# Weights streamed in pairs of chunks: one 1 MB load into two slots in place of two 512 KB loads

## The reference

```python
def first_block(x, ...):
    h = rms_norm(x, norm_mix_g[l])
    proj = h @ w_in[l]
    q, k, v, xr, gr, sc_b, sc_c, sc_x, g_pre = jnp.split(proj, offs, axis=-1)
    ...
    x = x + (g_a * y_a + g_b * y_b + g_c * y_c) @ w_out[l]
    h = rms_norm(x, norm_mlp_g[l])
    x = x + jnp.square(jax.nn.relu(h @ w_mlp_up[l])) @ w_mlp_down[l]
    return rms_norm(x, final_g)

def hybrid_layer(x, ...):
    h = rmsnorm(x, g_mix) @ w_in
    ...
    x = x + jnp.concatenate([y_ssd, y_att], axis=-1) @ w_out
    u = rmsnorm(x, g_mlp) @ w_up
    return x + jnp.square(jax.nn.relu(u)) @ w_down
```

## Time and profile before

| | |
|---|---|
| median of three runs | 2666.14 us (2665.62 to 2667.29) |
| the profiled execution | 2667.68 us, its span 2666.0 us |
| TensorE busy | 2656.8 us of the span |
| DVE, ACT busy | 1988.2 us, 1369.1 us |
| granted clock of TensorE | 0.999 |
| read from HBM | 505.08 MB, 191 GB/s over the span |

### The profile page before, as it was taken

One profiled execution on the slowest core, in us unless ns is written; L12 is line 12 of the kernel. 1 busy time (PEld: TensorE's weight loads), 2 busy tenths in 40 slices (PEclk: granted clock), 3 DMA queues, 4 the chain that ended last, 5 costly groups with the idle time before them and its releaser, 6 DMA issues.

```text
span 2666.0 us, 39598 instructions
## 1 busy us (share of the span) xinstructions
PE 2656.8 (100%) x13478; PEld 2243.8 (84%) x13478; DVE 1988.2 (75%) x2876; ACT 1369.1 (51%) x1865; POOL 30.3 (1%) x64
## 2 busy tenths in 40 slices
PE   9999999999999999999999999999999999999999
PEld 7888888888888888888888888888788888888887
DVE  5687876555555778798797577878787977879886
ACT  6455555444444554555554454456555555455453
POOL 0100000000000000000000000000000000000000
PEclk9999999999999999999999999999999999999999
DMA  7655556666665566566566555545555665656565
GB/s 275 227 173 188 185 169 195 207 198 194 204 192 186 177 197 202 185 195 199 187 207 203 189 178 172 175 151 189 171 173 189 199 197 189 205 188 195 186 202 175
DMA packets 141721, 511.06 MB, mean 192 GB/s; under 512 B 16134, under 2 KB 16439, under 8 KB 141464
## 3 DMA queue, kind: packets, MB, share of 16 engines
q1 hardware_dynamic: 136312, 493.86, 57.4%
q0 software_dynamic: 3840, 12.86, 1.5%
q10 hardware_dynamic: 1440, 2.62, 0.3%
HBM read 505.08 MB, written 4.21 MB: 191 GB/s over the span
## 4 chain that ended last, share of the span: by engine, by line
PE 94%; DVE 4%; DMA 1%; ACT 1%; issue 1%; SPq 0%; ACTq 0%; DVEq 0%
PE acc L1952 26%; PE acc L1953 13%; PE acc L1967 5%; PE acc L1984 4%; PE acc L1986 4%; PE acc L1985 4%; PE pS L1984 3%; PE pT L1986 3%; PE pS L1986 3%; PE pT L1984 3%; PE pS L1985 3%; PE pT L1985 3%; PE acc L1968 2%; PE pO L1984 1%; PE pO L1985 1%; PE pO L1986 1%
## 5 line engine op out<-in xcount | busy, mean ns | idle before, releaser
L1104 DVE TENSOR_TENSOR wlo<-raw,whi 128x1024 fp32r<-128x1024 f32 x938 | 1144.3, 1223 | 456.3 <-ACT whi L614 450.5
L614 ACT ACTIVATE whi<-raw 128x1024 fp32r<-128x1024 f32 x938 | 990.5, 1057 | 802.4 <-PE pT L1986 246.7
L1952 PE MATMUL acc<-a_w,whi 128*128 128x512 f32 x2944 | 1046.2, 400 | 0.1
L1953 PE MATMUL acc<-a_w,wlo 128*128 128x256 f32 x2944 | 827.3, 281 | 0.0
L1952 PEld LDWEIGHTS acc<-a_w,whi 128*128 128x128 f32 x2944 | 553.6, 188 | 137.8 <-issue 0.8
L1953 PEld LDWEIGHTS acc<-a_w,wlo 128*128 128x128 f32 x2944 | 556.6, 189 | 0.7
L1967 PE MATMUL acc<-a_w,whi 128*128 128x512 f32 x592 | 214.8, 405 | 0.0
L1968 PE MATMUL acc<-a_w,wlo 128*128 128x256 f32 x592 | 165.9, 280 | 0.0
L825 ACT ACTIVATE t<-acc 128x256 f32<-128x256 f32 x128 | 49.1, 383 | 176.8 <-PE acc L1953 175.1
L1967 PEld LDWEIGHTS acc<-a_w,whi 128*128 128x128 f32 x592 | 111.4, 188 | 27.0 <-issue 2.0
L1500 DVE TENSOR_TENSOR t<-acc,t 128x256 f32<-128x256 f32 x128 | 54.1, 423 | 79.2 <-ACT t L825 79.0
(11 more groups left out here) (496 smaller groups left out, 3962.5 us busy)
## 6 DMA issues: line engine op xcount, KB each, us to landing
raw<-stream SPq DMA_DIRECT2D x938, 512.0 KB, 3.4
gbias<-gateb POOLq DMA_DIRECT2D x12, 256.0 KB, 3.8
X<-x_rows POOLq DMA_DIRECT2D x4, 512.0 KB, 6.8
bias_scratch<-brow POOLq DMA_DIRECT2D x8, 256.0 KB, 5.7
q<-bias_scratch POOLq DMA_DIRECT2D x8, 256.0 KB, 4.0
out<-X ACTq DMA_DIRECT2D x8, 256.0 KB, 5.2
xF<-x SPq DMA_DIRECT2D x6, 256.0 KB, 6.9
bias<-bias_scratch POOLq DMA_DIRECT2D x8, 128.0 KB, 3.6
```

Of the source, the lines that this page charges most:

```text
L614: A(whi[:, slot, :], raw[:, slot, :], ACT.Copy).then_inc(s.hi_done, 1)
L1104: TT(wlo[:, slot, :], raw[:, slot, :], whi[:, slot, :].bitcast(F32), SUB).then_inc(s.lo_done, 1)
L1952: MM(ps, wh, wide[:, k0 + k, :], start=start and k == 0, stop=False, skip_group_check=True)
L1953: last = MM(ps[:, 0:T], wl, wide[:, k0 + k, 0:T], start=False, stop=not start and k == KC - 1, skip_group_check=True)
```

## The change

From chunk 4 on SP loads two chunks with one DMA of 1 MB, into slots 0 and 1 or 2 and 3, and waits for the subtraction of the chunk that lay in the second of the two slots. One semaphore for each pair of slots (`pair_landed`) tells of the landing; ACT's conversions of both chunks and the sums of DVE wait for it. The first four chunks are still loaded one by one. The number of chunks, the ring, the conversions and the products stay as they are.

```diff
+        pair_landed = [ctx.enter_context(nc.semaphore(f"pair_landed{k}")) for k in range(NSLOT // 2)]
...
+            def load_pair(c, slot):
+                sp.dma_start(raw[:, slot:slot + 2, :], stream[ds(c, 2)].rearrange("a p c -> p a c")).then_inc(pair_landed[slot // 2], 16)
+
             whole = CHUNKS // NSLOT
             with sp.Fori(1, whole) as i:
-                for k in range(NSLOT):
-                    sp.wait_ge(s.lo_done, i * NSLOT + (k - NSLOT + 1))
-                    load(i * NSLOT + k, k)
-            for c in range(whole * NSLOT, CHUNKS):
-                sp.wait_ge(s.lo_done, c - NSLOT + 1)
-                load(c, c % NSLOT)
+                for k in range(0, NSLOT, 2):
+                    sp.wait_ge(s.lo_done, i * NSLOT + (k - NSLOT + 2))
+                    load_pair(i * NSLOT + k, k)
+            for c in range(whole * NSLOT, CHUNKS, 2):
+                sp.wait_ge(s.lo_done, c - NSLOT + 2)
+                load_pair(c, c % NSLOT)
...
-                act.wait_ge(landed[slot], c.div(NSLOT).times(16).value(16))
+                if c.least() < NSLOT:
+                    act.wait_ge(landed[slot], 16)
+                else:
+                    act.wait_ge(pair_landed[slot // 2], c.div(NSLOT).times(16).value())
...
-                for e in range(2):
-                    dve.wait_ge(landed[slot + e], 16 * ((c + e) // NSLOT + 1))
+                dve.wait_ge(pair_landed[slot // 2], 16 * (c // NSLOT))
```

## The result

The change makes the kernel slower: 2681.31 us (median of five, 2679.04 to 2683.93) against 2666.14. The ratio is 1.0058, interval 1.0043 to 1.0073. That is outside the range that was forecast, 2665 to 2674, and on the side of rival A, though by another road than A's.

A forecast was written before the change was run, and what follows sets the result against it. TensorE, busy 2656.8 of 2666.0 us, was taken as the bound. Costs of 1.8 us at six crossings and 0 elsewhere were added to the median 2666.1, giving 2667.9, so 2668.0; range 2665.0 to 2674.0.

The forecast's parts named there:

- rival A: All pair loads: the 1 MB load lands late, over 0.2% slower from 5.2 us landing (2671.5), 2692 at 6.5; chance 0.15.
- What bounds the kernel: Whole program: TensorE busy 2656.8 of 2666.0 us at full clock; load changes can only be hidden or make it wait.
- L = 4.6: Pair loads on SP's queue: time from issue to landing of 1 MB taken as 4.6 us, ends 4.4 and 6.5.
- The slope of 6 us for each us of L: Six half changes in the down-projections: each further us from issue to landing costs 6 us more.
- The crossings: Change from a group's first half to its second, six times: late pairs delay DVE's run and TensorE, 1.8 us in all.
- a few tenths vanish: Within a half of the down-projections: TensorE has about 3 us in hand, so small delays disappear.
- The second loop: Successive block pairs in the same slots: landing time + 5.4 against TensorE's 10.2 us; DVE falls back over 4.8 us landing.
- Ordinary stretches: nothing: Judged on an up-projection stretch of the MLP: pair lands 1.05 us early, before TensorE's 5.9 us cover is touched; cost nothing.
- The start: 0, up to 2 us: Chunks 4 to 15: full queue, bytes decide; cost 0, up to 2 us if the first pairs fall behind.
- rival B: The start: squares of X later than reckoned, TensorE waits at 51.94; 2670, still within 0.2%; chance 0.05.
- The bound on conversion 12: The start: chunk 13 lands no later than 38.60, so ACT's conversion of chunk 12 moves by at most 2.7 us.
- D: All pairs: no different from two loads back to back, landing 4.5 us, sum 1.2, 2667.3; chance 0.76 together with the forecast.

The follow-up runs named there:

- e2: Against the changed kernel, each pair's 1 MB issued as two 512 KB loads, still under one joint semaphore; 2677.46 us, ratio 1.0047.
- e6: Against the changed kernel, the pair at each of the six crossings loaded by two single loads, 6 of 467 split; 2676.51 us, ratio 1.0041.
- e9: Against the kernel before, 1 MB loads in the two MLPs alone and not at the six crossings, 250 of 256 pairs; 2666.80 us, ratio 1.0004.
- e5: Against the changed kernel, single loads in both MLPs, pairs kept for chunks 4 to 303 and 560 to 681; 2674.65 us, ratio 1.0031.
- e7: Against the changed kernel, chunks 568 to 573, at the begin of the second layer's mixing, loaded singly; 2676.65 us, ratio 1.0040.
- e1: Against the changed kernel, same trigger, but two 512 KB loads back to back, each with its own semaphore; 2668.57 us, ratio 1.0013.
- e3: Against the changed kernel, the host lays a pair's two chunks so that each partition's 8 KB lie together in memory; 2680.63 us, ratio 1.0054.

## Where the prediction was right and where it failed

- *What bounds the kernel*: right. TensorE's busy time did not move, and only waits could be added.
- *L = 4.6*: failed by 0.3, a term that was mis-sized. Two loads back to back do complete 4.59 us after the first issue, so the sum of rows (3.2 to 3.4, and 1.3) was sound for two loads; one DMA of 1 MB takes 4.9 (4.8 packed). Its ends, 4.4 and 6.5, held it, but the sum was made at 4.6. The slope of 6 us for each us of L would have given 3.6 us at 4.9. That L is not what failed most is shown by e2, with 4.6 us and 11.8 us lost.
- *The crossings*: the mechanism and the place were right, the price was 1.8 and is 5.1, by the growth of the weight loads' wait (2.8 to 7.9) and by the steps in TensorE's delay alike, 4.8 by e6. Beside L the failed sentence is that within a half "a few tenths vanish": they stay (0.42, 0.44, 0.44). The second loop, L + 5.4 against 10.2, was written down under A, with 4.8 as the point from which DVE falls back. L is 4.9. The 0.45 us that a late `sums` leaves pass through `lo_done` into the next trigger.
- *"Ordinary stretches: nothing"*: right for what was called so, the MLPs outside the crossings (e9, 1.0004). It failed as a sum over the program, and this is the step that failed most: 8.9 of 15.2 us lie outside the MLPs (e5), where the prediction had 0. It took one stretch of the up-projection, 1.05 us early, for all that is not a block product. The first projection and the mixing have side work behind each conversion. There the subtractions are late already (lo of 565 to 567), so the trigger is late, and the cover that counts is not the 5.9 us until TensorE needs the chunk but that of `sm_t`, 0.05 us before. Chunk 570 had to be usable 3.15 us after its trigger there, so that even L = 4.6 would have cost 1.5 us. A wait's length is not its price either: the sum had no term for the clock behind a wait, some 1.4 us here. The price was 4.7 us at one chunk (e7) and 6.6 before chunk 304 in the changed kernel's trace, the start included.
- *The start: 0, up to 2 us*: it cost 2.6 us in the changed kernel's trace, but rival B, the late squares, is only 0.8 of it (in e5, with a wait of 2.1 us and the clock behind it, 4.0). The other 1.8 are TensorE's own waits for `wlo` at chunks 4 and 8, at which the prediction did not look. The bound on conversion 12, at most 2.7 us later, did not hold either: it took chunk 13 to land as before, at 38.0, and the pair landed at 40.7, so that the conversion started 4.8 us later, at 40.68. What costs at the start is the joint wait: up to the end of chunk 15 e1 loses nothing after chunk 0, and e2, with the same loads under one semaphore, 3.0 us. Pairs 8/9 to 14/15 took 6.5 to 8.1 us to land with X's loads beside them, where the single loads of these chunks took up to 6.9 before.
- *Rivals*: A was right in sign and in naming a late landing, wrong in the threshold: 5.2 us was not needed, because two thirds of the loss lie outside the place on which A's price rested. Its 6.5 us came in single landings, not as a rule, though one of them, at chunk 570, stands at the costliest place. By the figure that the Trainium skill gives for 1 MB, 6.15 us, the landing would have been some 1.2 us too long; it is given for another queue. That the estimate made from it, 2682, lies beside the measured 2681.3 is luck. D is refuted as a rival: two loads under one semaphore cost 11.8 us (e2), not 1.2, and one DMA costs some 4 more.

## What to carry to other kernels

The cover of a late transfer is not the distance to its own consumer but the least slack of everything that stands behind its first user on that engine's queue; look for it at every stage's border, not in one typical stretch. A joint semaphore makes the first half of a transfer as late as the second; where the ring is short, splitting the few loads at the tight places gives much of the loss back (here nine pairs of 467 gave 6.6 us of 15, and the 150 pairs before the first MLP another 6). When a loop of trigger, landing and use comes within tenths of the period of the consumer (10.3 against 10.2 us here), a delay in it stays.

## What the runs showed of the hardware

One DMA of 1 MB from SP's queue lands 4.9 us after its issue, two of 512 KB issued 0.53 us apart land 3.31 and 4.59 us after the first issue. The median hides what matters where the margin is small: one in twenty of the 467 loads took over 6.0 us, up to 8.3. The pair 570/571, with the next one issued 3.2 us behind it, took 5.5 to 6.5 us in all four kernels that load it with one DMA (e5, e3, the changed one, e6). Putting the two 4 KB runs of a partition side by side took 0.1 us off. TensorE's granted clock fell to 1.2 GHz for 3.4 us behind all four waits of 2.9 us and more, one of which thus cost 4.7 for its 3.3. It did so behind some waits of 2.1 to 2.6 us and not behind others, and behind none of 1.7 us or less. And 136 us of ScalarE's waiting for loads (e9) cost nothing that can be measured, where no work stood behind it that TensorE wanted soon.
